# Four layers on one core: position biases of the first layer as loaded tables, and both parts of a weight as one moving operand

## The reference, cut to what matters

```python
s = s - slope_kg * dist.astype(jnp.float32)
s = jnp.where(valid[None, :, None, None], s, -jnp.inf)
```

```python
blocks = t[:, tok_idx] + pe[:, None, :]
flat = blocks.transpose(0, 1, 3, 2, 4).reshape(B, n_cmp, G, CMP_BLOCK * DK)
return jax.nn.silu(flat @ w1) @ w2
```

## Time and profile before

| what | us |
|---|---|
| median of 3 runs | 985.57 |
| lowest, highest | 985.16, 1723.88 |
| the profiled execution, its own time | 987.59 |
| its span, first to last instruction | 985.8 |

### The profile page before, as it was taken

The page is one execution under the profiler, slowest core; times in us unless marked ns, Lnnn a source line. Parts: engine busy times, 40 slices in busy tenths (PEclk is TensorE's granted clock), DMA queues, the critical chain, the costliest instruction groups (busy, mean ns, idle before and its releaser), DMA issues.

```text
span 985.8 us, 14227 instructions
## 1 busy us (share of the span) xinstructions
PE 956.7 (97%) x5636; PEld 805.9 (82%) x5636; DVE 637.2 (65%) x1142; ACT 559.2 (57%) x924; POOL 137.4 (14%) x170
## 2 busy tenths in 40 slices
PE   5998999999999999999999999999999999999997
PEld 4875788888888777688888888999978899988865
DVE  4767687773446456568775444766668667467884
ACT  5676565543434666655545342655596446277772
POOL 0657000000000000000000025254013001311100
PEclk9999999999999999999999999999999999999999
DMA  9722445545554424236555565234232743331201
GB/s 347 275 88 86 172 171 175 196 180 208 182 185 157 171 86 135 80 130 217 202 177 203 182 221 199 87 128 150 108 128 86 276 137 138 125 115 44 87 22 43
DMA packets 21922, 150.30 MB, mean 152 GB/s; under 512 B 2528, under 2 KB 2656, under 8 KB 4448
## 3 DMA queue, kind: packets, MB, share of 16 engines
q1 hardware_dynamic: 21856, 149.40, 42.5%
HBM read 148.35 MB, written 1.05 MB: 152 GB/s over the span
## 4 chain that ended last, share of the span: by engine, by line
PE 85%; ACT 7%; DVE 5%; POOL 2%; issue 1%; DMA 0%; SPq 0%; ACTq 0%; DVEq 0%
PE bank L191 18%; PE bank L193 17%; PE bank L192 17%; PE bank L1165 12%; PE bank L1166 6%; ACT w_hi L157 2%; PE bank L931 1%; DVE w_lo L161 1%; PE bank L2288 1%; PE bank L2312 1%; PE bank L763 1%; PE bank L1606 1%; PE bank L2297 1%; PE bank L955 1%; PE bank L944 1%
## 5 line engine op out<-in xcount | busy, mean ns | idle before, releaser
L161 DVE TENSOR_TENSOR w_lo<-raw,w_hi 128x2048 fp32r<-128x2048 f32 x122 | 280.7, 2304 | 141.1 <-ACT w_hi L157 141.0
L157 ACT ACTIVATE w_hi<-raw 128x2048 fp32r<-128x2048 f32 x136 | 259.4, 1911 | 109.0 <-PE bank L193 109.0
L1165 PE MATMUL bank<-h,w_hi 128*128 128x512 f32 x512 | 181.2, 396 | 0.0
L1166 PE MATMUL bank<-h,w_lo 128*128 128x256 f32 x512 | 144.4, 282 | 0.0
L191 PE MATMUL bank<-h,w_hi 128*128 128x256 f32 x448 | 129.5, 289 | 0.7 <-DVE nsa_kcv L2642 0.7
L192 PE MATMUL bank<-h,w_hi 128*128 128x256 f32 x448 | 125.2, 279 | 0.0
L193 PE MATMUL bank<-h,w_lo 128*128 128x256 f32 x448 | 125.0, 279 | 0.0
L1165 PEld LDWEIGHTS bank<-h,w_hi 128*128 128x128 f32 x512 | 96.2, 188 | 23.4 <-issue 0.2
L191 PE MATMUL bank<-w_hi,mlp_u_hi 128*128 128x512 f32 x256 | 100.6, 393 | 0.0
L193 PE MATMUL bank<-w_hi,mlp_u_lo 128*128 128x512 f32 x256 | 100.5, 393 | 0.0
L192 PE MATMUL bank<-w_lo,mlp_u_hi 128*128 128x512 f32 x256 | 99.7, 389 | 0.0
(11 more groups left out here) (391 smaller groups left out, 1654.8 us busy)
## 6 DMA issues: line engine op xcount, KB each, us to landing
raw<-in_chunks SPq DMA_DIRECT2D x136, 1024.0 KB, 4.8
xres<-in_x SPq DMA_DIRECT2D x2, 512.0 KB, 5.5
raw<-in_chunks SPq DMA_DIRECT2D x2, 512.0 KB, 7.0
out<-final_xn SPq DMA_DIRECT2D x2, 512.0 KB, 2.6
ml_z<-in_ml SPq DMA_DIRECT2D x1, 896.0 KB, 6.2
even_const<-in_even SPq DMA_DIRECT2D x1, 576.0 KB, 14.9
small<-in_small SPq DMA_DIRECT2D x1, 559.5 KB, 13.0
final_gain<-in_fnorm SPq DMA_DIRECT2D x1, 512.0 KB, 3.6
```

Source lines behind the costliest of these rows:

```text
L157: act.activation(w_hi[slot][:, :], raw[slot][:, :], ACT.Copy).then_inc(hi_ready, 1)
L161: dve.tensor_tensor(w_lo[slot][:, :], raw[slot][:, :], w_hi[slot][:, :].bitcast(F32), ALU.subtract).then_inc(lo_ready, 1)
L1165: pe.matmul(dst[:, :], w_hi[slot][:, cols], h[:, k, :, :], start=(k == 0), stop=False)
L1166: last = pe.matmul(dst[:, 0:S], w_lo[slot][:, cols], h[:, k, 0, :], start=False, stop=(k == KT - 1))
```

## The change

First layer: the host lays out the finished biases of all eight pairs (distance times slope plus table), as eight tables of 128 x 768 float32, 384 KB each. POOL's queue loads them, three before it copies the first sinks and the others as tiles come free; three tiles rotate in place of four. POOL computes nothing for them, and the masks on DVE wait for the landing. The tables of before and SP's load of them are gone.

Fourth layer: `w_hi` and `w_lo` of a slot lie in one tile, so that a matmul can take the same 128 columns of both as one moving operand of 256. Each step of the compression is then two matmuls: the high part by both (256 columns of the bank), and the low part by `w_hi` (128 columns). The hidden rows are 65 x 256 in two halves, and `turn_hidden` adds the halves while it turns them, by two accumulating products with the identity. The later results take other columns of the bank.

```diff
@@ constants and the ring
-CONST_EVEN = [("dist", 3 * P), ("ln_count", 3 * P), ("window", 3 * P)]
+EVEN_PAIRS = [(i + 4) % 8 for i in range(8)]
...
-    w_hi = [sb(ctx, f"w_hi{i}", [P, CHUNK], F32R) for i in range(RING)]
-    w_lo = [sb(ctx, f"w_lo{i}", [P, CHUNK], F32R) for i in range(RING)]
+    w_both = [sb(ctx, f"w_hi_lo{i}", [P, 2, CHUNK], F32R) for i in range(RING)]
+    w_hi, w_lo = ([w[:, x, :] for w in w_both] for x in range(2))
@@ Attention.mask
-            if b["biased"]:
-                dve.wait_ge(self.bias_ready.sem, self.bias_ready.at(i + 1))
+            if b["bias_loaded"] is not None:
+                dve.wait_ge(*b["bias_loaded"])
@@ tiles of the first layer
-    econst = sb(es, "even_const", [P, even_n])
-    N_BIAS = 4
+    N_BIAS = 3
+    bias_loaded = [sem(f"bias_loaded{i}") for i in range(N_BIAS)]
...
+        both = dict(tile=tile, q=q_even[:, tile, :], mask=[bias[i % N_BIAS][:, e, :] for e in range(2)],
+                    bias_loaded=(bias_loaded[i % N_BIAS], 16 * (i // N_BIAS + 1)))
@@ block.sync
-            sp.dma_start(econst[:, :], even_in).then_inc(econst_loaded, 16)
@@ block.gpsimd
+            pool.wait_ge(lo_ready, 3)
+            for i in range(N_BIAS):
+                pool.dma_start(bias[i][:, :, :].rearrange("p e w -> p (e w)"), even_in[i]).then_inc(bias_loaded[i], 16)
             pool.wait_ge(qg_ready, 1)
-            pool.wait_ge(econst_loaded, 16)
             for i in range(2):
                 e_att.sinks(pool, i)
-            for i, b in enumerate(e_att.pairs):
-                if i >= 2 and i < 4:
-                    e_att.sinks(pool, i)
-                if i >= N_BIAS:
-                    pool.wait_ge(e_att.maxed.sem, e_att.maxed.at(4 * (i - N_BIAS + 1)))
-                for e in range(2):
-                    n = 2 * b["tile"] + e
-                    slope, table = (slopes[8 + n], "ln_count") if n < 8 else (slopes[n - 8], "window")
-                    pool.tensor_scalar(bias[i % N_BIAS][:, e, :], ec("dist"), -float(np.float32(slope)), None,
-                                       ALU.mult).then_inc(bias_scaled, 1)
-                    pool.wait_ge(bias_scaled, 2 * i + e + 1)
-                    last = pool.tensor_tensor(bias[i % N_BIAS][:, e, :], bias[i % N_BIAS][:, e, :], ec(table), ALU.add)
-                last.then_inc(e_att.bias_ready.sem, 1)
+            for i in range(N_BIAS, len(e_att.pairs)):
+                if i - N_BIAS + 2 < 4:
+                    e_att.sinks(pool, i - N_BIAS + 2)
+                pool.wait_ge(e_att.maxed.sem, e_att.maxed.at(4 * (i - N_BIAS + 1)))
+                pool.dma_start(bias[i % N_BIAS][:, :, :].rearrange("p e w -> p (e w)"), even_in[i])\
+                    .then_inc(bias_loaded[i % N_BIAS], 16)
@@ Nsa
-            self.hid = [sb(stack, f"nsa_hid{m}", [N_WIN + 2, P]) for m in range(2)]
+            self.hid = [sb(stack, f"nsa_hid{m}", [N_WIN + 2, 2 * P]) for m in range(2)]
@@ Nsa.compress
-                last = product(pe, bank[self.CMP[m]][0:N_WIN + 2, 0:P], self.kc[m][0][:, tok], self.kc[m][1][:, tok],
-                               w_hi[slot][:, w], w_lo[slot][:, w], jj == 0, jj == CMP_BLOCK // 2 - 1)
+                end = jj == CMP_BLOCK // 2 - 1
+                if end:
+                    self.lower_part(pe, m, slot, tok, w)
+                last = pe.matmul(bank[self.CMP[m]][0:N_WIN + 2, 0:2 * P], self.kc[m][0][:, tok], w_both[slot][:, :, w],
+                                 start=jj == 0, stop=end)
+                if not end:
+                    self.lower_part(pe, m, slot, tok, w)
             last.then_inc(chunk_used, 1)
 
+        def lower_part(self, pe, m, slot, tok, w):
+            pe.matmul(bank[self.CMP[m]][0:N_WIN + 2, 0:P], self.kc[m][1][:, tok], w_hi[slot][:, w], start=False, stop=False)
+
         def turn_hidden(self, pe, m):
+
             pe.wait_ge(self.hid_ready.sem, self.hid_ready.at(m + 1))
-            pe.transpose(bank[self.CMP[m]][:, P:P + N_WIN + 2], self.hid[m][:, :], ident[0:N_WIN + 2, 0:N_WIN + 2])\
-                .then_inc(self.hid_turned.sem, 1)
+            for x in range(2):
+                last = pe.matmul(bank[self.CMP[m]][:, S:S + N_WIN + 2], self.hid[m][:, x * P:(x + 1) * P],
+                                 ident[0:N_WIN + 2, 0:N_WIN + 2], start=x == 0, stop=x == 1)
+            last.then_inc(self.hid_turned.sem, 1)
@@ Nsa.act
-            act.activation(self.hid[0][:, :], bank[self.CMP[0]][0:N_WIN + 2, 0:P], ACT.Copy).then_inc(self.hid_ready.sem, 1)
+            act.activation(self.hid[0][:, :], bank[self.CMP[0]][0:N_WIN + 2, 0:2 * P], ACT.Copy).then_inc(self.hid_ready.sem, 1)
```

More of the change, by code:

```diff
@@ L1311, in build @@
     ey_lo = sb(es, "even_y_lo", [P, KT, S], F32R)
-    qg_ready, vb_kept, bias_scaled = sem("even_qg_ready"), sem("even_vb_kept"), sem("bias_scaled")
-    def ec(name):
-        return econst[:, slice(*even_at[name])]
-    slopes = [2.0 ** (-8.0 * (n + 1) / HEADS) for n in range(HEADS)]
+    qg_ready, vb_kept = sem("even_qg_ready"), sem("even_vb_kept")
     pairs = []
-    for i in range(8):
-        tile = (i + 4) % 8
+    for i, tile in enumerate(EVEN_PAIRS):
         heads = (2 * tile, 2 * tile + 1)
-        both = dict(tile=tile, q=q_even[:, tile, :], mask=[bias[i % N_BIAS][:, e, :] for e in range(2)], biased=True)
+        both = dict(tile=tile, q=q_even[:, tile, :], mask=[bias[i % N_BIAS][:, e, :] for e in range(2)],
+                    bias_loaded=(bias_loaded[i % N_BIAS], 16 * (i // N_BIAS + 1)))
         if i < 4:
@@ L1336, in build @@
     e_att = Attention(es, "eat", pairs, ey_hi, ey_lo, (6, 7), (4, 5))
-    e_out = OutPhase("eout", E_OUT, (0, 1, 2, 3), [(i + 4) % 8 for i in range(8)], e_att, m0_turned, eo_stats)
+    e_out = OutPhase("eout", E_OUT, (0, 1, 2, 3), EVEN_PAIRS, e_att, m0_turned, eo_stats)
     es.close()
@@ L2239, in compressed_values @@
             for g in range(GROUPS):
-                last = pe.matmul(bank[self.CMP[1]][0:2 * PAD, S + g * DH:S + (g + 1) * DH],
+                last = pe.matmul(bank[self.CMP[1]][0:2 * PAD, g * DH:(g + 1) * DH],
                                  self.hid_v[:, g, :, :].rearrange("p e c -> p (e c)"), sm("w2_v"), start=True, stop=True)
@@ L2569, in act @@
             act.wait_ge(chunk_used, c0 + self.W1 + 1)
[L2570 removed]
+            act.activation(self.hid[0][:, :], bank[self.CMP[0]][0:N_WIN + 2, 0:2 * P], ACT.Copy).then_inc(self.hid_ready.sem, 1)
             round_for(act, c0 + 7)
             act.wait_ge(chunk_used, c0 + self.W1 + 2)
[L2573 removed]
+            act.activation(self.hid[1][:, :], bank[self.CMP[1]][0:N_WIN + 2, 0:2 * P], ACT.Copy).then_inc(self.hid_ready.sem, 1)
             for m in range(2):
                 act.wait_ge(self.hid_turned.sem, self.hid_turned.at(m + 1))
[L2576 removed]
+                act.activation(self.bias[:, m:m + 1], bank[self.CMP[m]][:, S + N_WIN + 1:S + N_WIN + 2], ACT.Copy)\
                     .then_inc(self.hid_bias.sem, 1)
@@ L2579, in act @@
                 if m == 0:
-                    act.activation(self.hid_k[:, :], bank[self.CMP[m]][:, P:P + N_WIN], ACT.Silu, bias=self.bias[:, m:m + 1])\
+                    act.activation(self.hid_k[:, :], bank[self.CMP[m]][:, S:S + N_WIN], ACT.Silu, bias=self.bias[:, m:m + 1])\
                         .then_inc(self.hid_kept.sem, 1)
@@ L2583, in act @@
             act.wait_ge(self.cleared.sem, self.cleared.at(1))
[L2584 removed]
+            by_group = bank[self.CMP[1]][:, S:S + GROUPS * WIN].rearrange("p (g c) -> p g c", g=GROUPS)[:, :, 0:N_CMP]
             for e in range(2):
@@ L2594, in act @@
                 last = act.activation(self.kcmp[rows, :, e, 0:N_CMP],
-                                      bank[self.CMP[0]][rows, S:S + GROUPS * WIN].rearrange("p (g c) -> p g c", g=GROUPS)[:, :, 0:N_CMP],
+                                      bank[self.CMP[0]][rows, 0:GROUPS * WIN].rearrange("p (g c) -> p g c", g=GROUPS)[:, :, 0:N_CMP],
                                       ACT.Copy)
@@ L2601, in act @@
                 last = act.activation(self.vcmp[rows, :, e * DH:(e + 1) * DH],
-                                      bank[self.CMP[1]][rows, S:S + GROUPS * DH].rearrange("p (g d) -> p g d", g=GROUPS), ACT.Copy)
+                                      bank[self.CMP[1]][rows, 0:GROUPS * DH].rearrange("p (g d) -> p g d", g=GROUPS), ACT.Copy)
             last.then_inc(self.cmp_kept.sem, 1)
@@ L3401, in shape_constants @@
     }
+    ln_count = np.where(ok & (count > 0), np.log(np.maximum(count, 1)), NEG).astype(f)
+    window = np.where(ok & (dist < 128), 0.0, NEG).astype(f)
+    slopes = [f(2.0 ** (-8.0 * (n + 1) / HEADS)) for n in range(HEADS)]
+    even = np.stack([np.concatenate([dist.astype(f) * -(slopes[8 + n] if n < 8 else slopes[n - 8])
+                                     + (ln_count if n < 8 else window) for n in (2 * tile, 2 * tile + 1)], 1)
+                     for tile in EVEN_PAIRS])
     def pack(table):
         return np.concatenate([full[n].astype(f).reshape(P, w) for n, w in table], 1)
```

(2 more changed lines are left out.)

12 lines of the change are left out of this document (2 added, 10 removed).

## The result

The kernel after took 979.85 us in the median of 4 executions (978.60 to 981.15), the kernel before 985.37 beside it: a ratio of 0.9937, with a 95% interval from 0.9923 to 0.9951. The gain of 0.6% is clear of the noise and under the 2% from which a measurement here is told from no change. The forecast was 979.2, with a range from 977.2 to 984.0. Run again beside the experiments, the kernel after took 978.65 (978.0 to 979.2).

The account below looks back on a forecast made before the run. The prediction took TensorE (PE), busy 956.7 of 985.8 us, to bound the kernel. Savings of 3.6 us (bias tables) and 2.8 (compression), 6.4 in all, from the median 985.57 gave 979.2 us, range 977.2 to 984.0.

Parts of the forecast that it names:

- The sum: Whole kernel: 3.6 us from the bias tables plus 2.8 from the compression, 6.4 us saved; chance 0.56.
- Part 1: First layer: without POOL's bias arithmetic DVE's multiplies end earlier and PE's three waits for them go; 3.6 us saved.
- C: Rival: half the gain is spent at the next wait, for ACT or DVE; 982.4 us, chance 0.08.
- The loads: First layer: eight table loads from POOL's queue cost nothing, as DVE's half remainder covers later issues; other end 3.6 us.
- The cover of 14 us: First layer: time between the fifth pair's table issue and its mask in the faster schedule, enough for the table to land.
- D: Rival: tables land late and masks wait, passing the gain from a 17.7 us landing; 990.2 us at 20, chance 0.06.
- Part 2: Fourth layer's compression: 32 steps go from 0.345 to 0.2325 us, saving 3.6, less 0.8 for the turns: 2.8 us.
- A1: Rival, compression: the operand in two runs of 128 streams at the slow rate, 0.22 us; 982.5 us, chance 0.08.
- A2: Rival, compression: a step's time follows its 384 columns and stays 0.345 us, turns added; 982.8 us, chance 0.05.
- The turns: Fourth layer: turning hidden rows by two plain products in place of one transpose, twice, costs 0.8 us.
- B: Rival, first layer: POOL's DMA issues hold DVE up as its arithmetic did; 982.8 us, chance 0.14.
- The clock: Whole kernel: the clock column stands at 1.00, the 2.4 GHz level, in both stretches shown, so no part is a clock.

Follow-up runs that it names:

- experiments 1 to 3: Five kernels: each part of the change alone, POOL's arithmetic put back, tables loaded by SP's queue, and two bias tiles; medians 980.08 to 984.25 us.
- pool_dummy: The kernel after, with POOL also doing 16 scalings and 16 additions on a scratch tile nobody reads; 984.25 us, ratio 0.9981 to before.
- by_offset: The kernel after with second-layer products moved into PE's two waits, the old compression, and split tokens laid out so stationary columns lie side by side; 974.42 us, ratio 0.9874.
- loads_sp: The kernel after, with the eight bias tables loaded by SP's queue in place of POOL's; 980.63 us, ratio 0.9943 to before.
- two_tiles: The kernel after, with two rotating bias tiles in place of three; 980.08 us, ratio 0.9923 to before.
- part2_only: The kernel before with the new compression alone, POOL still computing the bias tables; 984.13 us, ratio 0.9978 to before.

## Why the prediction was right, point by point

**The sum.** 6.4 us was forecast from two terms, 3.6 and 2.8; the stages give 3.8 and 2.9. The executions of before at a granted clock of 0.999 or 1.000 (nine, beside experiments 1 to 3) have a median of 984.7, the six of after one of 978.7: 6.1 us, with the start-up of stage A, which varies by a microsecond, in it. That 979.85 came within 0.7 us of 979.2 is partly luck: it is a median of four, two at a mean clock of 0.995 to 0.996 (980.6 and 981.2) and two at 0.999 to 1.000 (978.6 and 979.1). The stages are the better test of the sum.

**Part 1** was right in its mechanism, and the named turns in their size. "... the three are worth 3.2 + 3 x 0.16 = 3.7 us" is what they gave, 1.46 + 0.79 + 1.46 = 3.71. "I take 3.6, because the DVE work would end only just in time" was the wrong caution. Around them the prediction's upper side and its rival C both came true in part: smaller delays gave some 0.7 more, and the new wait of 0.6, for DVE's low part of the attention's output, took it back. It had not been named. pool_dummy shows the cause by its own.

**The loads** cost nothing in B, as forecast, though not for the reason given: two of the five later issues did not fall ahead of the multiplies but among them, and the multiplies took 1.04 us all the same. The cover of 14 us was sound, and so was its use against D: 3.4 us is far from the 17.7 from which D would have decided. (D's 5.3 us a pair takes all three delays off the way from the third turn to the seventh, but the third pair's lies ahead of it; the masks of the last four pairs stand 5.5 apart. It moves nothing here.) By the "DVE blocks DMA" trap of the Trainium skill ("SBUF — State Buffer", "SBUF: two separate sides") the prediction had put some 2.5 us on a table, as an estimate; the traces show 0.1 between the two queues, with DVE as busy. With the lock that the same section of the Trainium skill describes the traces agree, and pool_dummy is its cleanest number here: 1.0 to 2.1 us.

**Part 2** was right in its sum and wrong in its reason. The step "one product with 256 moving columns and one with 128 ... so a step goes from 0.345 to 0.1175 + 0.115 = 0.2325" gave 0.231. But I read the earlier trace rows as a price of an instruction with few columns. It is the price of a weight load from spaced columns, 0.115, and a step after is two of these: it stays at 0.23 with 192 columns in place of 256, and falls only when the loads change. Why the starts inside a step stand 0.17 and 0.06 apart, and not evenly, isn't shown. The two prices lie 2% apart by chance, so the forecast could not fail on it. What it cost was the better edit. All float32r products of 128 columns in the trace before have this stationary operand, and those of 256 have others; nothing in them told columns streamed from columns loaded.

**A1** falls: an operand in two runs of 128 streams in at most 0.17. **A2** falls as a forecast for this kernel, but its rule comes near where the load is no bound. There 128 columns take 0.061 us (by_offset). The Trainium skill ("TensorE: Matmul & The Clock Gate", "Back-to-back issue gap") has 56 ns for them as the gap of a product by itself and about 81 in a stream of loads and products; the trace, a stream, lies 5 ns above the first. The prediction had set that rule aside because "the row has 115 ns for 128 columns, double the page's". Double was the thing to explain. The same page of the Trainium skill ("LDWEIGHTS (loading the stationary operand)") puts a load at P / 1.2 ns, so an estimated 54 for 65 columns; side by side the trace has at most 60, spaced 115. The Trainium skill ("SBUF — State Buffer", in "Door 1: The DMA port swizzle") says that accesses which go to a new line of 16 bytes each time pay a penalty; the columns here lie 64 bytes apart, and the run with 65 side by side agrees.

**The turns** were put at 0.8, from 0.13 an instruction; they cost 0.66. Rival **B** falls by loads_sp and **D** by two_tiles. **C** came true in small: 0.6 us of part 1 was spent at the new wait, not half of a part, and nothing behind the stages B, F and G.

**The clock.** "The clock column stands at 1.00 in both stretches shown ... so no part of the answer is a clock" was wrong: two stretches of 10 us were read, of a hundred. The profiled execution was 2.0 us above the median, and a fall that cost 3.0 us stands in its second layer. Working from the median took that out of the forecast without knowing it, which was luck and not a reading.

## What to carry to other kernels

When a row costs twice what its columns should, find out which operand it waits for before choosing an edit: here merging two products took away every third slow weight load (2.9 us), and laying out the stationary operand side by side made them all fast (5.1 us). An engine off the critical path can still cost by computing beside one that is on it, where a DMA issue in its place cost nothing. For differences under 1%, compare stages of two traces and the clock of each stretch, not medians of four executions.

## What the hardware showed that was not expected

- Products of 128 float32r columns whose stationary operand has 65 columns 64 bytes apart go at 0.115 us each; with 65 side by side, or 33 spaced, at 0.060.
- Behind two pauses of PE of 1.0 to 1.1 us within some 3 us, the granted clock fell from 2.4 to 1.2 GHz in some executions (45 of 101 by their mean clock, and none of 12 with the pauses filled or worked away), and the fall cost 3.0 us, or 1.5 in part2_only; in the fourth layer a fall behind a pause of 1.7 us cost 1.0 in four of the profiled executions.
- A load of 384 KB lands in 3.4 us from POOL's queue and 3.3 from SP's; POOL spends 0.54 to 0.60 us on each of the later issues, SP 0.33.
